# Entry of an expert stage: weights asked for before the search, turns through six banks, upper and lower parts in halves

## The chip, the cores and the metric

One core of a Trainium2 chip. The metric is the device time of one execution in microseconds. TensorE is called PE in the profile, VectorE DVE, ScalarE ACT, GpSimd POOL, and SyncE SP.

## What is computed

One step of a backbone with one layer: 128 context tokens and 2,048 latent tokens of width 1,024. The layer ends in an expert stage in which each of 16 experts chooses its tokens:

```python
cap = CAPACITY_FACTOR * L // N_EXPERTS
affinity = jax.nn.softmax(jnp.einsum('bld,de->ble', h, w_router).astype(jnp.float32), axis=-1)
gate, idx = lax.top_k(jnp.swapaxes(affinity, 1, 2), cap)
xe = jax.vmap(lambda hb, ib: hb[ib])(h, idx)
hid = jax.nn.silu(jnp.einsum('becd,edf->becf', xe, w_gate)) * jnp.einsum('becd,edf->becf', xe, w_up)
ye = jnp.einsum('becf,efd->becd', hid, w_down) * gate[..., None].astype(h.dtype)
return jax.vmap(lambda ib, yb: jnp.zeros((L, D), yb.dtype).at[ib.reshape(-1)].add(yb.reshape(-1, D)))(idx, ye)
```

Here `h` is the token's row after its norm, scaled and shifted. Every expert takes 256 latent tokens and 16 context tokens. All of it is float32.

## The kernel before

The program is a row of stages, each a block with one instruction stream for each engine, and all engines meet at its end. Three matter here. The stage `mixer` stores the normed rows (`normed`) and the rows before the experts (`x2`) to HBM. The stage `selection` finds, by a search of digits on VectorE with small sums on TensorE, which tokens each expert takes, and writes each token's place in `g.pos`. The stage `experts` does the rest; it runs over the 16 experts, the first and the last two written out and the others in a loop.

**An expert in the steady state.** A float32 product is made of three: the weights are split into an upper part `whi` and a lower part `wlo`, the rows into `xhi` and `xlo`, and TensorE adds `whi*xhi`, `whi*xlo` and `wlo*xhi`. The weights of an expert come in 12 chunks of 1 MB (4 of the gate matrix and 4 of the up matrix in turn, then 4 of the down matrix). SyncE's queue loads a chunk into one of three buffers `raw`; it is asked for when `wlo` of the chunk three before it is written. ScalarE copies `raw` to `whi`, VectorE writes `wlo` as `raw` less `whi`; both are rings of four. A product (`product`, 24 matmuls) works off 128 columns of a chunk. For each of 8 tiles `ft` of the hidden width there is a gate product and an up product, then come 8 down products.

**The rows.** For expert `e` VectorE marks in `one_hot(e)`, with 16 compares, which token stands at which place; TensorE adds that up in `compact(e)` (32 small matmuls); VectorE reads the sums in `indices(e)` and writes the row numbers `idx` and the gates. GpSimd's `gather(e)` is two indirect transfers of 512 KB each from `normed` into `xg`; from expert 1 on it also waits until the turns of the expert before are done with `xg`. In `rows_in(e, kk)` TensorE turns (transposes) 128 columns `kk` of the 256 rows, two transposes into a bank of PSUM, and ScalarE (even `kk`) or VectorE (odd `kk`) copies the bank scaled and shifted to `xf`. `rows_high` on ScalarE then copies `xf` to `xhi` in one instruction of 2,048 elements, and `rows_low` on VectorE writes `xlo` in one. In the steady state `rows_in(e + 1, ft)` stands behind the two products of tile `ft` of expert `e`, so TensorE's first turn of expert 1 stands behind its first two products.

**The context rows.** The rows of all 16 experts (256 in all) are gathered at once into `yo`, turned in `context_in` and kept in `kept_c`; each expert copies its 16 from there behind its 256 latent rows.

**The entry.** Ahead of the first product of expert 0 all this happens in the open. TensorE's order: `compact(0)`, `compact_context`, `compact(1)`, then the turns of expert 0 through the two banks `ps_x` (each pair waits until the copy of two pairs before is done) and those of the context rows through the four banks `ps_r`. VectorE's order: `one_hot(0)`, the context's marks, `indices(0)`, `indices_context`, `one_hot(1)`, `split(0, 0)` (the lower part of chunk 0), `indices(1)`, copies, `split(0, 1)`, `rows_low(0)`, `split(0, 2)`. ScalarE's: the upper parts of chunks 0 and 1, copies, `rows_high(0)`, the upper part of chunk 2. SyncE asks for chunks 0 to 2 as the stage begins. The first product waits for `xlo_done`.

The functions as they stand, with their line numbers:

## Time and profile before

| | |
|---|---|
| median of 3 runs | 2353.88 us (2350.2 to 2355.96) |
| profiled execution | 2351.41 us, its span 2349.5 us |
| granted clock of TensorE, mean | 0.958 |
| busy: TensorE, VectorE, ScalarE, GpSimd | 93%, 57%, 43%, 8% |
| DMA | 398.66 MB, mean 170 GB/s |
| `experts` begins | 1048.9 us |
| first product of expert 0 | 1074.96 us |

The trace has one execution. Its times count from the start of the span. A row of the timeline has start and length, engine, line, the tile written and those read, and in brackets how long the engine stood idle before it and what ended that. "SPq" and "POOL DMA_INDIRECT" are issues of transfers, not the transfers. PEclk is the granted clock of TensorE as a share of 2.4 GHz.

### The profile page before, as it was taken

What the parts mean: (1) busy time and instruction counts of PE and PEld (TensorE: products, weight loads), DVE (VectorE), ACT (ScalarE), POOL (GpSimd) and SP (SyncE); (2) the same over time, 40 slices, a digit from 0 to 9 for tenths busy, and PEclk for the clock granted to TensorE, in tenths of its full rate; (3) what the DMA queues carried; (4) which work ended last, traced back from release to release, by engine and by line L of the source; (5) the groups of instructions that cost most, each with busy time, mean ns of one, the idle gap of its engine ahead of it and who ended that gap; (6) DMA issues with size and microseconds to landing.
All of it is one profiled execution on the core that took longest, in us unless ns stands there. A gap on an engine that the chain in (4) does not pass through costs nothing.

```text
span 2349.5 us, 39243 instructions
## 1 busy us (share of the span) xinstructions
PE 2174.3 (93%) x15527; PEld 2010.7 (86%) x15527; DVE 1349.8 (57%) x2079; ACT 999.8 (43%) x1725; POOL 196.0 (8%) x276
## 2 busy tenths in 40 slices
PE   4899999996699999828999999999999999999995
PEld 2878888885588888628999999999999999999995
DVE  2656543407577777475565556555655656565564
ACT  3642221224355555214444444434444444344653
POOL 0000000000011111010000000000000000000112
PEclk8999999998799999858999999999999999999998
DMA  8533343137343444115665666565656665666794
GB/s 288 177 125 133 131 146 125 56 119 239 109 131 129 137 148 148 63 44 189 189 207 166 201 194 202 171 190 187 208 175 188 192 210 167 190 192 201 249 311 158
DMA packets 320348, 398.66 MB, mean 170 GB/s; under 512 B 11631, under 2 KB 273279, under 8 KB 318207
## 3 DMA queue, kind: packets, MB, share of 16 engines
q1 hardware_dynamic: 288990, 287.21, 38.0%
q0 software_dynamic: 24912, 97.53, 13.5%
q10 hardware_dynamic: 6352, 12.65, 1.5%
q8 instruction: 62, 1.02, 0.2%
q14 instruction: 32, 0.25, 0.0%
HBM read 320.22 MB, written 77.14 MB: 169 GB/s over the span
## 4 chain that ended last, share of the span: by engine, by line
PE 48%; DMA 3%; DVE 1%; ACT 1%; issue 1%; POOL 1%; ACTq 0%; DVEq 0%; POOLq 0%
PE experts_ps_r L2380 45%; PE experts_ps_x L2360 1%; PE experts_ps_o L2370 1%; DMA out_y_sample<-experts_xg 1%; DMA out_y_sample<-experts_xf 1%; DMA out_y_sample<-experts_onehot 1%; PE experts_ps_i L2298 0%; ACT experts_whi L2456 0%; DMA x<-experts_yo,experts_idx 0%; ACT experts_junk L2489 0%; DVE experts_wlo L2603 0%; DMA experts_xg<-x,experts_idx 0%; DMA experts_xg<-normed,experts_idx 0%; POOL experts_raw L2264 0%; DVE experts_onehot L2614 0%
## 5 line engine op out<-in xcount | busy, mean ns | idle before, releaser
L2603 DVE TENSOR_TENSOR experts_wlo<-experts_raw,experts_whi 128x2048 fp32r<-128x2048 f32 x192 | 439.9, 2291 | 393.6 <-ACT experts_whi L2456 393.6
L2380 PE MATMUL experts_ps_r<-experts_xhi,experts_whi 128*128 128x272 f32 x2048 | 603.4, 295 | 7.9 <-DVE experts_xlo L2654 5.5
L2380 PE MATMUL experts_ps_r<-experts_xhi,experts_wlo 128*128 128x272 f32 x2048 | 594.1, 290 | 0.0
L2380 PE MATMUL experts_ps_r<-experts_xlo,experts_whi 128*128 128x272 f32 x2048 | 590.8, 288 | 0.0
L2380 PEld LDWEIGHTS experts_ps_r<-experts_xhi,experts_whi 128*128 128x128 f32 x2048 | 387.0, 189 | 8.6 <-DVE experts_xlo L2654 5.7
L2380 PEld LDWEIGHTS experts_ps_r<-experts_xlo,experts_whi 128*128 128x128 f32 x2048 | 387.7, 189 | 0.0
L2380 PEld LDWEIGHTS experts_ps_r<-experts_xhi,experts_wlo 128*128 128x128 f32 x2048 | 386.6, 189 | 0.0
L2456 ACT ACTIVATE experts_whi<-experts_raw 128x2048 fp32r<-128x2048 f32 x192 | 366.1, 1907 | 13.9 <-DMA experts_raw<-in_w_gate 13.1
L2380 PE MATMUL experts_ps_r<-experts_hhi,experts_whi 128*128 128x272 f32 x1024 | 301.3, 294 | 2.0 <-DVE experts_hlo L2767 1.9
L2380 PE MATMUL experts_ps_r<-experts_hhi,experts_wlo 128*128 128x272 f32 x1024 | 296.2, 289 | 0.0
L2380 PE MATMUL experts_ps_r<-experts_hlo,experts_whi 128*128 128x272 f32 x1024 | 294.7, 288 | 0.0
L521 PE MATMUL front_ps<-front_hhi,front_whi 128*128 128x384 f32 (+1 forms) x640 | 236.2, 369 | 0.0
L521 PE MATMUL front_ps<-front_hlo,front_whi 128*128 128x384 f32 (+1 forms) x640 | 230.7, 360 | 0.0
L521 PE MATMUL front_ps<-front_hhi,front_wlo 128*128 128x384 f32 (+1 forms) x640 | 230.6, 360 | 0.0
L2546 ACT ACTIVATE experts_hhi<-experts_hid 128x272 fp32r<-128x272 f32 x128 | 55.2, 431 | 353.8 <-DVE experts_hid L2764 353.8
L2380 PEld LDWEIGHTS experts_ps_r<-experts_hhi,experts_whi 128*128 128x128 f32 x1024 | 192.6, 188 | 5.8 <-DVE experts_hlo L2767 5.6
L2380 PEld LDWEIGHTS experts_ps_r<-experts_hlo,experts_whi 128*128 128x128 f32 x1024 | 193.1, 189 | 0.2 <-issue 0.2
L2380 PEld LDWEIGHTS experts_ps_r<-experts_hhi,experts_wlo 128*128 128x128 f32 x1024 | 192.6, 188 | 0.0
L659 ACT ACTIVATE front_u<-front_ps 128x128 f32<-128x128 f32 (+2 forms) x90 | 40.2, 469 | 247.6 <-PE front_ps L521 227.1
L521 PEld LDWEIGHTS front_ps<-front_hhi,front_whi 128*128 128x128 f32 x640 | 120.8, 189 | 25.4 <-ACT front_u L659 12.6
L521 PEld LDWEIGHTS front_ps<-front_hlo,front_whi 128*128 128x128 f32 x640 | 120.9, 189 | 11.9 <-issue 1.0
L521 PEld LDWEIGHTS front_ps<-front_hhi,front_wlo 128*128 128x128 f32 x640 | 120.7, 189 | 11.8
(474 smaller groups left out, 3169.4 us busy)
## 6 DMA issues: line engine op xcount, KB each, us to landing
experts_raw<-in_w_gate SPq DMA_DIRECT2D x64, 1024.0 KB, 5.0
experts_raw<-in_w_up SPq DMA_DIRECT2D x64, 1024.0 KB, 5.0
experts_raw<-in_w_down SPq DMA_DIRECT2D x64, 1024.0 KB, 5.1
shared_whalf<-in_w_ada SPq DMA_DIRECT2D x16, 1024.0 KB, 5.1
ssd_mz<-mixed SPq DMA_DIRECT2D x17, 768.0 KB, 7.7
mixed<-front_acc POOLq DMA_DIRECT2D x9, 1024.0 KB, 4.2
resid<-early_xin POOLq DMA_DIRECT2D x17, 512.0 KB, 3.2
ssd_xs<-resid SPq DMA_DIRECT2D x17, 512.0 KB, 4.0
```

Source lines behind the costliest of these rows:

```text
L521: mm = pe.matmul(ps[:, out, 0:n], wt[buf][:, kk, :], h[:, kk, t0:t0 + n], start=(kk == 0 and q == 0), stop=(kk == KD - 1 and q == 2))
L659: ins = act.activation(dst_u[:, uo:uo + pn], ps[:, bank_of(s), po:po + pn], func)
L2360: ins = pe.transpose(ps_x[:, kk % 2, P * a:P * a + P], xg[:, a, P * kk:P * kk + P], g.ident[:, :])
L2370: ins = pe.transpose(ps_o[:, P * q:P * q + P], yt[:, 4 * half + q, P * a:P * a + P], g.ident[:, :])
L2380: mm = pe.matmul(dst, w[:, c % RING, kk, cols], r[:, kk, :], start=(kk == 0 and q == 0), stop=(kk == KD - 1 and q == 2))
L2456: act.activation(whi[:, c % RING, :, :], raw[:, c % RAW, :, :], ACT.Copy).then_inc(whi_done, 1)
L2546: act.activation(hhi[:, ft, :], hid[:, ft % 2, :], ACT.Copy).then_inc(hhi_done, 1)
L2603: dve.tensor_tensor(wlo[:, c % RING, :, :], raw[:, c % RAW, :, :], whi[:, c % RING, :, :].bitcast(F32), ALU.subtract).then_inc(wlo_done, 1)
```

## The change

Three things at the entry of `experts`, and one in `indices`.

1. The buffers `raw` and their semaphores are made ahead of `selection`, and SyncE asks for the chunks 0 to 2 in `selection`, as soon as the last rows of `mixer` are stored. `experts` starts with chunk 3.
2. The turns of expert 0 and of the context rows go through one rotation of six banks (`start_bank`: the two of `ps_x`, then the four of `ps_r`), all 8 pairs of expert 0 first, then the 8 of the context; a pair waits for the copy of six pairs before (`bank_free`).
3. The upper and the lower part of expert 0's rows are made in two halves of 1,024 elements (`start_high`, `start_low`), the first between the copies; the context's piece comes by itself (`context_high`, `context_low`). `indices(1)` and `split(0, 1)` stand behind that on VectorE.
4. `indices` writes `idx` ahead of the gates' sums, for every expert.

```diff
         @block.sync
         def _(sp):
+            for sem, value in g.rows_stored:
+                sp.wait_ge(sem, value)
+            for c in range(RAW):
+                w = io[("w_gate", "w_up")[c % 2]][0].rearrange("e (k p) f -> e p k f", p=P)
+                sp.dma_start(g.raw[:, c, :, :], w[0, :, :, CH * (c // 2):CH * (c // 2) + CH]).then_inc(g.w_loaded[c], 16)
...
+        def start_bank(turn):
+            b = turn % 6
+            return ps_x[:, b, :] if b < 2 else ps_r[:, b - 2, :]
...
+            def bank_free(turn):
+                old = turn - 6
+                if 0 <= old < KD:
+                    pe.wait_ge((xf_act, xf_dve)[old % 2], old // 2 + 1)
+                elif old == KD:
+                    pe.wait_ge(ctx_scaled, 1)
+                elif old == KD + 1:
+                    pe.wait_ge(ctx_chain, C_SCALED + 1)
+
+            def start_rows(kk):
+                if kk == 0:
+                    pe.wait_ge(gathered, 32)
+                bank_free(kk)
+                for a in range(2):
+                    ins = pe.transpose(start_bank(kk)[:, P * a:P * a + P], xg[:, a, P * kk:P * kk + P], g.ident[:, :])
+                ins.then_inc(xin_done, 1)
...
             compact(0)
             compact_context()
             compact(1)
-            for kk in range(0, KD + 4, 2):
-                for b in range(2):
-                    if kk < KD:
-                        rows_in(0, kk + b)
-                for b in range(2):
-                    if kk >= 4:
-                        context_in(kk - 4 + b)
+            for kk in range(KD):
+                start_rows(kk)
+            for kk in range(KD):
+                start_context(kk)
             loops(body, pe)
...
+            def start_high(half):
+                act.wait_ge(xf_act, 2 * half + 2)
+                act.wait_ge(xf_dve, 2 * half + 2)
+                kk = slice(4 * half, 4 * half + 4)
+                act.activation(xhi[:, kk, 0:CAP_L], xf[:, kk, :], ACT.Copy).then_inc(xhi_done, 1)
...
             split(0, 0, True)
             split(0, 1, True)
-            for kk in range(0, KD + 4, 2):
-                if kk < KD:
-                    rows_in(0, kk)
-                if kk >= 4:
-                    context_in(kk - 4)
-            rows_high(0)
+            for half in range(2):
+                for kk in (0, 2):
+                    rows_in(0, 4 * half + kk)
+                start_high(half)
+            for kk in range(0, KD, 2):
+                context_in(kk)
+            context_high(0)
             split(0, 2, True)
...
                 idxs.link(dve.tensor_copy(got[:, :, 0:NV], ps_i[:, :, 0:NV]))
+                dve.scalar_tensor_tensor(idx[0][:, :], got[:, :, 0], float(P), got[:, :, 1], ALU.mult, ALU.add
+                                         ).then_inc(idx_done, 1)
                 idxs.link(dve.tensor_tensor(gate[0][:, :], got[:, :, 3], got[:, :, 4], ALU.add))
                 dve.tensor_tensor(gate[0][:, :], gate[0][:, :], got[:, :, 2], ALU.add)
-                dve.scalar_tensor_tensor(idx[0][:, :], got[:, :, 0], float(P), got[:, :, 1], ALU.mult, ALU.add
-                                         ).then_inc(idx_done, 1)
...
+            def start_low(half):
+                dve.wait_ge(xhi_done, half + 1)
+                kk = slice(4 * half, 4 * half + 4)
+                dve.tensor_tensor(xlo[:, kk, 0:CAP_L], xf[:, kk, :], xhi[:, kk, 0:CAP_L].bitcast(F32), ALU.subtract)
...
             one_hot(1)
             split(0, 0)
+            rows_in(0, 1)
+            rows_in(0, 3)
+            rows_in(0, 5)
+            start_low(0)
+            rows_in(0, 7)
+            context_in(1)
+            start_low(1)
+            for kk in (3, 5, 7):
+                context_in(kk)
+            dve.wait_ge(xhi_done, START)
+            context_low(0)
+            split(0, 1)
             indices(1)
-            for kk in range(1, KD + 4, 2):
-                if kk < KD:
-                    rows_in(0, kk)
-                if kk >= 4:
-                    context_in(kk - 4)
-            split(0, 1)
-            rows_low(0)
             split(0, 2)
             loops(body, dve)
```

What this makes of TensorE's order, from the sums of `compact(0)` (`ps_i`) to the first matmul of the first product. Before:

```order
L2298 MATMUL experts_ps_i<-experts_val_e,experts_onehot 128x5 x32
L2306 MATMUL experts_ps_o<-kept_vals,experts_onehot_c 128x80 x2
L2298 MATMUL experts_ps_i<-experts_val_e,experts_onehot 128x5 x32
L2360 MATMUL experts_ps_x<-kept_ident,experts_xg 128x128 x12
L2318 MATMUL experts_ps_r<-kept_ident,experts_yo 128x128 x4
L2360 MATMUL experts_ps_x<-kept_ident,experts_xg 128x128 x4
L2318 MATMUL experts_ps_r<-kept_ident,experts_yo 128x128 x12
L2380 MATMUL experts_ps_r<-experts_xhi,experts_whi 128x272
```

And now:

```order
L2311 MATMUL experts_ps_i<-experts_val_e,experts_onehot 128x5 x32
L2319 MATMUL experts_ps_o<-kept_vals,experts_onehot_c 128x80 x2
L2311 MATMUL experts_ps_i<-experts_val_e,experts_onehot 128x5 x32
L2337 MATMUL experts_ps_x<-kept_ident,experts_xg 128x128 x4
L2337 MATMUL experts_ps_r<-kept_ident,experts_xg 128x128 x8
L2337 MATMUL experts_ps_x<-kept_ident,experts_xg 128x128 x4
L2345 MATMUL experts_ps_r<-kept_ident,experts_yo 128x128 x8
L2345 MATMUL experts_ps_x<-kept_ident,experts_yo 128x128 x4
L2345 MATMUL experts_ps_r<-kept_ident,experts_yo 128x128 x4
L2406 MATMUL experts_ps_r<-experts_xhi,experts_whi 128x272
```

The turns of the context rows (`yo`) no longer stand between those of expert 0 (`xg`), and both are spread over `ps_x` and `ps_r`.

ScalarE, from the upper parts of chunks 0 and 1 (`whi`) to that of chunk 2. Before:

```order
L2456 ACTIVATE experts_whi<-experts_raw 128x2048 x2
L2460 ACTIVATE experts_xf<-experts_ps_x,kept_mod,kept_scale_m 128x256 x3
L2465 ACTIVATE experts_kept_c<-experts_ps_r,kept_mod,kept_scale_m 128x256
L2460 ACTIVATE experts_xf<-experts_ps_x,kept_mod,kept_scale_m 128x256
L2465 ACTIVATE experts_kept_c<-experts_ps_r,kept_mod,kept_scale_m 128x256 x3
L2532 ACTIVATE experts_xhi<-experts_xf 128x8x256
L2533 ACTIVATE experts_xhi<-experts_kept_c 128x8x16
L2456 ACTIVATE experts_whi<-experts_raw 128x2048
```

And now:

```order
L2479 ACTIVATE experts_whi<-kept_raw 128x2048 x2
L2484 ACTIVATE experts_xf<-experts_ps_x,kept_mod,kept_scale_m 128x256
L2484 ACTIVATE experts_xf<-experts_ps_r,kept_mod,kept_scale_m 128x256
L2560 ACTIVATE experts_xhi<-experts_xf 128x4x256
L2484 ACTIVATE experts_xf<-experts_ps_r,kept_mod,kept_scale_m 128x256
L2484 ACTIVATE experts_xf<-experts_ps_x,kept_mod,kept_scale_m 128x256
L2560 ACTIVATE experts_xhi<-experts_xf 128x4x256
L2489 ACTIVATE experts_kept_c<-experts_ps_r,kept_mod,kept_scale_m 128x256 x2
L2489 ACTIVATE experts_kept_c<-experts_ps_x,kept_mod,kept_scale_m 128x256
L2489 ACTIVATE experts_kept_c<-experts_ps_r,kept_mod,kept_scale_m 128x256
L2566 ACTIVATE experts_xhi<-experts_kept_c 128x8x16
L2479 ACTIVATE experts_whi<-kept_raw 128x2048
```

One upper part of the rows (`xhi` from `xf`) of 8x256 has become two of 4x256, one of them ahead of half of the copies; the context's piece (8x16) is last as before.

VectorE, from the last instruction of `indices(1)` before (the row numbers `idx`) to the lower parts of chunks 2 and 3. Before:

```order
L2628 SCALAR_TENSOR_TENSOR experts_idx<-experts_got 128x2
L2648 TENSOR_SCALAR experts_xf<-experts_ps_x,kept_scale_m,kept_mod 128x256 x3
L2697 TENSOR_SCALAR experts_kept_c<-experts_ps_r,kept_scale_m,kept_mod 128x256
L2648 TENSOR_SCALAR experts_xf<-experts_ps_x,kept_scale_m,kept_mod 128x256
L2697 TENSOR_SCALAR experts_kept_c<-experts_ps_r,kept_scale_m,kept_mod 128x256 x3
L2603 TENSOR_TENSOR experts_wlo<-experts_raw,experts_whi 128x2048
L2653 TENSOR_TENSOR experts_xlo<-experts_xf,experts_xhi 128x8x256
L2654 TENSOR_TENSOR experts_xlo<-experts_kept_c,experts_xhi 128x8x16
L2603 TENSOR_TENSOR experts_wlo<-experts_raw,experts_whi 128x2048 x2
```

And now, from the second half of `xlo` on:

```order
L2694 TENSOR_TENSOR experts_xlo<-experts_xf,experts_xhi 128x4x256
L2740 TENSOR_SCALAR experts_kept_c<-experts_ps_r,kept_scale_m,kept_mod 128x256
L2740 TENSOR_SCALAR experts_kept_c<-experts_ps_x,kept_scale_m,kept_mod 128x256
L2740 TENSOR_SCALAR experts_kept_c<-experts_ps_r,kept_scale_m,kept_mod 128x256
L2697 TENSOR_TENSOR experts_xlo<-experts_kept_c,experts_xhi 128x8x16
L2637 TENSOR_TENSOR experts_wlo<-kept_raw,experts_whi 128x2048
L2668 COPY experts_idx<-experts_idx 128x2
L2669 COPY experts_gate<-experts_gate 128x2
L2659 COPY experts_got<-experts_ps_i 128x2x5
L2660 SCALAR_TENSOR_TENSOR experts_idx<-experts_got 128x2
L2662 TENSOR_TENSOR experts_gate<-experts_got 128x2
L2663 TENSOR_TENSOR experts_gate<-experts_gate,experts_got 128x2
L2637 TENSOR_TENSOR experts_wlo<-kept_raw,experts_whi 128x2048 x2
```

The lower part of chunk 1 (`wlo`) stood ahead of `xlo` and now stands behind it; the six instructions of `indices(1)` (two copies of `idx` and `gate`, `got`, `idx`, two sums) stood ahead of all copies and now stand behind that `wlo`. GpSimd's gather for expert 1 waits for the `idx` among them.

## Rows read from the trace of the kernel before

**Rows 1.** The page, part 1: engine, busy us, share of the span, instructions.

```profile
PE 2174.3 (93%) x15527; PEld 2010.7 (86%) x15527; DVE 1349.8 (57%) x2079; ACT 999.8 (43%) x1725; POOL 196.0 (8%) x276
```

**Rows 2.** TensorE's waits, 1082 to 2290 us: total us, times, longest us.

```profile
PE experts_ps_r L2380 <- DVE experts_wlo L2603: 2.5, 2, 2.2
PE experts_ps_r L2380 <- DVE experts_hlo L2767: 1.7, 1, 1.7
```

**Rows 3.** The timeline, 1054 to 1063 us: start, us, engine, line, instruction.

```profile
1054.10 1.91 ACT L2456 ACTIVATE experts_whi<-experts_raw 128x2048 fp32r<-128x2048 f32 x1 [13.11 <-DMA experts_raw<-in_w_gate]
...
1054.13 0.15 DVE L2628 SCALAR_TENSOR_TENSOR experts_idx<-experts_got 128x2 uint32<-128x2 f32 x1
...
1055.15 1.04 POOL L2196 DMA_INDIRECT experts_xg<-normed,experts_idx  x1 [50.16 <-DVE experts_idx L2628]
...
1056.77 1.91 ACT L2456 ACTIVATE experts_whi<-experts_raw 128x2048 fp32r<-128x2048 f32 x1 [0.76 <-DMA experts_raw<-in_w_up]
...
1056.89 3.30 DVE L2614 TENSOR_SCALAR experts_onehot<-kept_slots,experts_pos_e 128x256 bf16<-128x256 bf16 x16
...
1060.03 2.29 DVE L2603 TENSOR_TENSOR experts_wlo<-experts_raw,experts_whi 128x2048 fp32r<-128x2048 f32 x1
...
1060.25 1.01 PE L2298 MATMUL experts_ps_i<-experts_val_e,experts_onehot 128*128 128x5 bf16 x32 [6.30 <-DVE experts_onehot L2614]
...
1062.04 0.71 PEld L2360 LDWEIGHTS experts_ps_x<-kept_ident,experts_xg 128*128 128x128 f32 x4 [0.87 <-DMA experts_xg<-normed,experts_idx]
...
1062.77 0.56 ACT L2460 ACTIVATE experts_xf<-experts_ps_x,kept_mod,kept_scale_m 128x256 f32<-128x256 f32 x1 [4.08 <-PE experts_ps_x L2360]
```

**Rows 4.** The timeline, 1068 to 1075 us, up to the first product.

```profile
1068.31 0.95 POOL L2196 DMA_INDIRECT experts_xg<-normed,experts_idx  x1 [8.16 <-PE experts_ps_x L2360]
...
1068.44 1.70 DVE L2697 TENSOR_SCALAR experts_kept_c<-experts_ps_r,kept_scale_m,kept_mod 128x256 f32<-128x256 f32 x3 [0.24 <-PE experts_ps_r L2318]
...
1070.27 1.91 ACT L2532 ACTIVATE experts_xhi<-experts_xf 128x2048 fp32r<-128x2048 f32 x1 [0.55 <-DVE experts_kept_c L2697]
...
1072.41 2.29 DVE L2653 TENSOR_TENSOR experts_xlo<-experts_xf,experts_xhi 128x2048 fp32r<-128x2048 f32 x1
...
1072.50 0.37 SPq L2177 DMA_DIRECT2D experts_raw<-in_w_gate  x1
...
1074.62 0.28 DVE L2654 TENSOR_TENSOR experts_xlo<-experts_kept_c,experts_xhi 128x128 fp32r<-128x128 f32 x1
...
1074.96 0.59 PE L2380 MATMUL experts_ps_r<-experts_xhi,experts_whi 128*128 128x272 f32 x1 [5.47 <-DVE experts_xlo L2654]
```

**Rows 5.** DMA queues, 1056.8:1058.4, 1058.6:1061.6, 1069.8:1074.2: packets, MB, share of 16 engines.

```profile
q1 hardware_dynamic: 603, 0.62, 108.4%
...
q0 software_dynamic: 326, 1.21, 98.3%
...
q0 software_dynamic: 286, 1.05, 75.3%
```

**Rows 6.** Windows: stretch, busy us of each engine, PEclk, DMA share, GB/s.

```profile
990.00:1000.00 10.00, 10.00 (x48) 10.00 (x48) 3.11 (x9) 0.43 (x1) 2.52 (x9) 0.50 0.00 1
```

**Rows 7.** The timeline, first turns of expert 1, and expert 2's index and gather.

```profile
1082.72 0.38 PE L2360 MATMUL experts_ps_x<-kept_ident,experts_xg 128*128 128x128 f32 x2
...
1088.99 0.38 PE L2360 MATMUL experts_ps_x<-kept_ident,experts_xg 128*128 128x128 f32 x2
...
1149.08 0.15 DVE L2628 SCALAR_TENSOR_TENSOR experts_idx<-experts_got 128x2 uint32<-128x2 f32 x1
...
1149.51 0.95 POOL L2196 DMA_INDIRECT experts_xg<-normed,experts_idx  x1 [79.00 <-DVE experts_idx L2628]
```

**Rows 8.** Windows, 1070 to 1080 us, for the granted clock (PEclk).

```profile
1070.00:1072.00 2.00, 0.00 (x0) 0.00 (x0) 1.97 (x2) 1.73 (x1) 0.51 (x1) 0.94 0.88 254
1072.00:1074.00 2.00, 0.00 (x0) 0.00 (x0) 2.00 (x2) 2.00 (x3) 0.00 (x0) 0.50 0.88 275
...
1078.00:1080.00 2.00, 2.00 (x16) 2.00 (x15) 0.00 (x0) 0.11 (x1) 0.00 (x0) 0.85 0.92 290
```

More of the change, by code:

```diff
@@ L2159, in experts @@
         C_GATED = 4
+        START = 3
         C_SAVED, C_SSQ = 17, 25
@@ L2172, in body @@
                 for c in range(NCH):
+                    if first and c < RAW:
+                        continue
                     w, col = (wd, c - 8) if c >= 8 else ((wg, wu)[c % 2], c // 2)
-                    if not (first and c < RAW):
-                        hold(sp, settled, (wlo_done, e * NCH + (c - RAW + 1)))
+                    hold(sp, settled, (wlo_done, e * NCH + (c - RAW + 1)))
                     src = w[bass.ds(e, 1), :, :, CH * col:CH * col + CH].rearrange("o p k f -> (o p) k f")
@@ L2308, in compact_context, with start_context @@
                 mm.then_inc(ctx_turned, 1)
-            def context_in(kk):
+            def bank_free(turn):
[13 more added lines that the diff above has]
+                ins.then_inc(xin_done, 1)
+            def start_context(kk):
                 if kk == 0:
                     pe.wait_ge(ctx_moved, 32)
-                if kk >= 4 and kk % 2 == 0:
-                    pe.wait_ge(ctx_scaled, kk // 2 - 1)
-                elif kk >= 4:
-                    pe.wait_ge(ctx_chain, C_SCALED + kk // 2 - 1)
+                bank_free(KD + kk)
                 for h in range(2):
-                    ins = pe.transpose(ps_r[:, kk % 4, P * h:P * h + P], yo[:, h, P * kk:P * kk + P], g.ident[:, :])
+                    ins = pe.transpose(start_bank(KD + kk)[:, P * h:P * h + P], yo[:, h, P * kk:P * kk + P], g.ident[:, :])
                 ins.then_inc(ctx_turned, 1)
@@ L2356, in rows_in @@
                     pe.wait_ge(gathered, e * 32 + 32)
-                if not (first_tiles(e, 1) and kk < 2):
-                    pe.wait_ge((xf_act, xf_dve)[kk % 2], e * 4 + kk // 2)
+                pe.wait_ge((xf_act, xf_dve)[kk % 2], e * 4 + kk // 2)
                 for a in range(2):
@@ L2459, in rows_in @@
                 act.wait_ge(xin_done, e * 8 + (kk + 1))
-                act.activation(xf[:, kk, :], ps_x[:, 0, 0:CAP_L], ACT.Identity,
+                src = start_bank(kk) if first_tiles(e, 1) else ps_x[:, 0, :]
+                act.activation(xf[:, kk, :], src[:, 0:CAP_L], ACT.Identity,
                                scale=g.scale_m[:, kk, 1:2], bias=g.mod[:, SH_M + kk, 1:2]).then_inc(xf_act, 1)
@@ L2528, in rows_high, with context_high @@
                 act.wait_ge(xf_dve, e * 4 + 4)
+                act.activation(xhi[:, :, 0:CAP_L], xf[:, :, :], ACT.Copy)
+                context_high(e)
+            def start_high(half):
[3 more added lines that the diff above has]
+                act.activation(xhi[:, kk, 0:CAP_L], xf[:, kk, :], ACT.Copy).then_inc(xhi_done, 1)
+            def context_high(e):
                 if first_tiles(e, 1):
@@ L2647, in rows_in, with context_low @@
                 dve.wait_ge(xin_done, e * 8 + (kk + 1))
-                dve.tensor_scalar(xf[:, kk, :], ps_x[:, 1, 0:CAP_L], g.scale_m[:, kk, 1:2],
+                src = start_bank(kk) if first_tiles(e, 1) else ps_x[:, 1, :]
+                dve.tensor_scalar(xf[:, kk, :], src[:, 0:CAP_L], g.scale_m[:, kk, 1:2],
                                   g.mod[:, SH_M + kk, 1:2], ALU.mult, ALU.add).then_inc(xf_dve, 1)
             def rows_low(e):
-                dve.wait_ge(xhi_done, e + 1)
+                dve.wait_ge(xhi_done, e + START)
                 dve.tensor_tensor(xlo[:, :, 0:CAP_L], xf[:, :, :], xhi[:, :, 0:CAP_L].bitcast(F32), ALU.subtract)
+                context_low(e)
+            def start_low(half):
+                dve.wait_ge(xhi_done, half + 1)
+                kk = slice(4 * half, 4 * half + 4)
+                dve.tensor_tensor(xlo[:, kk, 0:CAP_L], xf[:, kk, :], xhi[:, kk, 0:CAP_L].bitcast(F32), ALU.subtract)
+            def context_low(e):
                 dve.tensor_tensor(xlo[:, :, CAP_L:ROWS], kept_c[:, :, bass.ds(e, 1), :].rearrange("p k o c -> p k (o c)"),
@@ L2696, in context_in @@
                 dve.wait_ge(ctx_turned, C_IN + kk + 1)
-                step(dve.tensor_scalar(kept_c[:, kk, :, :].rearrange("p e c -> p (e c)"), ps_r[:, kk % 4, 0:NE * CAP_C],
+                step(dve.tensor_scalar(kept_c[:, kk, :, :].rearrange("p e c -> p (e c)"), start_bank(KD + kk)[:, 0:NE * CAP_C],
                                        g.scale_m[:, kk, 0:1], g.mod[:, SH_M + kk, 0:1], ALU.mult, ALU.add),
@@ L2863, in build @@
         g.gm_rows = k.sb("gm_rows", [P, 2, D])
+        g.raw, g.w_loaded = k.sb("raw", [P, RAW, KD, CH]), k.sems("w_loaded", RAW)
         g.slots = k.sb("slots", [P, CAP_L], BF16)
```

8 lines of the change are left out of this document (4 added, 4 removed).

## The prediction

> **What bounds the kernel now.** I read the page first: TensorE works for 93% of the span [rows 1]. Then the waits of TensorE from 1082 us to 2290 us, the loop over the experts: two releasers, 4.2 us in all [rows 2]. So from the first products on TensorE is the bound, everything behind it follows at its pace, and what the change does to the time is by how much earlier TensorE runs once its stream is steady, that is behind the first rows of expert 1. The entry has one long wait: the first product stands still for 5.47 us until `xlo` is written and starts at 1074.96 [rows 4].
>
> Third view, the timeline of the entry. Its chain of last waits is: VectorE's 16 compares of `one_hot(1)` from 1056.89 to 1060.19; `compact(1)` on TensorE, 1060.25 to 1061.26; a gap of 0.78 us, which the landing of expert 0's gathered rows ends, and turns from 1062.04 [rows 3]; copies out of the turned rows, the last three of them context copies of VectorE, 1068.44 to 1070.14; the whole upper part on ScalarE, 1.91 us from 1070.27; the whole lower part on VectorE, 2.29 us from 1072.41, then its context piece at 1074.62; the product [rows 4]. From the first turn to the first product it is 12.9 us.
>
> **The weights, fetched early.** Three transfers of 1 MB leave the entry. ScalarE's 13.11 us and 0.76 us of waiting for them go [rows 3], but are worth nothing by themselves: ScalarE is through both upper parts at 1058.68 and has its first rows at 1062.77 [rows 3]. What they did cost is the queue: from 1056.8 to 1058.4 the 16 DMA engines move only weights, and the gathers (software queue) move from 1058.6 on, though the first was issued at 1055.15 [rows 3, 5]. The undisturbed gather of expert 1 is issued at 1068.31 and its megabyte is moved from 1069.8 to 1074.2, all but a few packets: 1.5 us to the first byte, 5.9 us from the first issue to the end [rows 4, 5]. So gather 0 now ends near 1055.15 − 0.28 (the index is written before the gate sums, two links earlier) + 5.9 = 1060.8, before `compact(1)` ends at 1061.26. The turns start there, 0.78 us earlier. At their new place, before the search, the transfers meet DMA engines that are idle from 990 to 1000, and VectorE works 3.11 of those 10 us [rows 6]; there I cost them at 0, and at 3.1 us if VectorE took twice as long beside them, which no row suggests.
>
> **The turns and the halves.** Transposes issue every 0.18 us (four in 0.71 us) [rows 3], a pair in 0.36. With six banks none of the first six pairs waits. Copies cost 0.56 us on ScalarE and 1.70 / 3 = 0.57 on VectorE [rows 3, 4]; a half of the upper part is taken as 1.91 / 2 = 0.96 or a little more, a half of the lower as 1.15 [rows 4]. First rows reach ScalarE 0.73 us after the first transpose [rows 3], so:
> - ScalarE: copy 0 at 1062.0, copy 2 at 1062.7; VectorE: `wlo` 0 until 1062.3 (now with no `indices(1)` behind it), copy 1 at 1062.4, copy 3 at 1063.1.
> - Upper half 0 from 1063.7 to 1064.7; ScalarE copies 4 and 6 until 1065.8. VectorE: copy 5 until 1064.4, lower half 0 from 1064.8 to 1065.9, copy 7 until 1066.5, context copy 1 until 1067.0.
> - Upper half 1 from 1066.5 to 1067.5, lower half 1 from 1067.55 to 1068.7, then context copies 3, 5, 7 on VectorE until 1070.4. ScalarE's context copies 0, 2, 4, 6 end at 1069.8 and lie beside them; turns 14 and 15 wait for context copy 0, done at 1068.1, and are not last.
> - Context piece of the upper part 0.3 us, of the lower one from 1070.8; the product follows 0.34 us after that start, as now (1074.62 to 1074.96) [rows 4]: **1071.15**.
>
> That is 3.8 us earlier: 0.8 from the turns' start, 3.0 from halves that lie beside the turns. The first product needs `wlo` 0 alone; the second needs `wlo` 1, now split behind `xlo`, 1071.0 to 1073.3, long before the first product (over 4 us at the low clock) ends. Chunk 4 of the weights is then asked for at 1073.3 in place of 1072.50 [rows 4]; its first product is the ninth, four pairs of 6.3 us [rows 7] behind the first.
>
> **What is late next.** `indices(1)` moved behind `split(0, 1)`. Before, gather 1 waited 8.16 us for the turns and was issued at 1068.31 [rows 4]. Now its index waits for VectorE: 1073.3 plus two small copies, `got` and the index, 0.15 to 0.2 us each, so the index starts at 1073.7; in the loop the gather follows 0.43 us behind (1149.08 to 1149.51) [rows 7]: **issued at 1074.15, 5.8 us later than before**. TensorE's third step, the first turn of expert 1, waits for it. In the trace of before that turn stands at 1082.72, 7.76 us behind the first product [rows 4, 7]; now TensorE is there at 1078.9. The gather alone would land at 1074.15 + 5.9 = 1080.05. But chunk 4, issued 0.85 us ahead of it, needs 2.7 us of all engines (0.62 MB in 1.6 us) [rows 5]; if the software queue stands back for it as it did at 1056.8, the first rows move from about 1077.3 and then 1 MB takes some 3.3 us (the four gathers moved 1.21 MB in 3.0) [rows 5]: 1080.6. I take 1080.6, since that queueing is what the trace shows. TensorE then waits 1.7 us.
>
> So the sum is not 3.8 us. Whatever the entry gives, TensorE goes on at the landing: 1082.72 − 1080.6 = 2.1 us. Bounds: 1080.05 gives 2.7 us; if chunk 5, asked for at 1076.4, shares the engines too, all three megabytes end near 1074.5 + 3 × 2.7 = 1082.6 and nothing is left of the gain.
>
> The Trainium skill says (DMA: Bandwidth & Descriptors, SWDGE vs HWDGE vs iDMA) that each DMA engine goes round-robin between its software and hardware queues. By that, gather 1 would share with chunk 4 and land about 1080.1, a gain of 2.6 us, or near 1082.6 if chunk 5 shares with it. The trace speaks against it at one place: no software packet in the 1.6 us of [rows 5].
>
> **The clock.** In the windows the granted clock is 0.94 from 1070 to 1072, 0.50 (1.2 GHz) from 1072 to 1074, and 0.85 from 1078 to 1080, back at 2.4 GHz some 3.5 us into the products [rows 8], and TensorE stood idle from the last turn, near 1069.5, to 1074.96. The low clock costs: first pair of products 7.76 us, the second with its turn 6.27 (1082.72 to 1088.99) [rows 4, 7], so 1.5 us and the turn, some 1.7. The new idle time before the products is about 2.7 us instead of 5.5. Were the clock still high there, TensorE would only reach the gather earlier and wait longer: worth nothing. What counts is whether it falls in the wait for gather 1: then up to 1.7 us are lost behind it. The Trainium skill warns of such waits in a stream of products (TensorE: Matmul & The Clock Gate, HAM oscillation). A wait of 1.7 us between 7.8 us of work and more work is short beside the idle time that lowered it here, so I leave it out of the sum.
>
> **Rivals.**
> - *Gather 1 is in time, or nearly* (landing by 1079.2): 3.6 us or so faster, about 2350.2. For it: the DMA engines have little else. Against it: even undisturbed it takes 5.9 us. Chance 0.13.
> - *The gather wait outruns the entry's gain* (the other side): it lands behind 1082.7, because both chunks go ahead of it or POOL starts as late as after the first index (1.02 us behind it, 1054.13 to 1055.15 [rows 3]), and the clock falls in the 3.8 us of waiting. At 1082.8 and with 1.7 us of low clock it is +1.8 us, 2355.7. It decides from a landing of 1082.7, or of 1081.0 with the clock low. Chance 0.17.
> - *The fetch does not do its work*, because `compact(1)` and not the gather starts the turns: it is worth 0.8 us at most in any case; without it the first product is at 1071.9 and the sum is the same, as the landing of gather 1 rules. It can't be told in the time. Chance 0.1, at 2351.8.
> - *Forecast*: 2.1 us faster. Chance 0.5. The rest, 0.1, is for what the moved buffer and the new places of waits do elsewhere.
>
> **How the numbers follow.** The profiled execution took 2351.41 us (span 2349.5 and 1.9 around it); by the sum it would take 2349.3. The median of the three runs is 2353.88, 2.5 us above it, so the forecast is 2353.9 − 2.1 = 2351.8. The three runs lie 5.8 us apart, so a median of three may be off by 2 us by itself. The range goes from 2348 (2350.2 less 2) to 2356 (2355.7). A measurement here tells about 0.3%, 7 us, from no change. The largest gain that any case has is 3.8 + 1.7 = 5.5 us, with the clock high from the first product and no wait; so faster by more than that has 0.04, slower 0.02, no difference 0.94.
>
> **What the new profile would show.** Right: no wait of ScalarE for weights at the entry; turns from 1061.3 on that clock; two half upper parts of about 1 us between the copies; first product 9.9 us behind the first turn; gather 1 issued 3 us behind the first product's start; TensorE idle 1 to 2.5 us at the first turn of expert 1, released by that gather; that turn 9.5 us behind the first product. Wrong: a gather that lands inside the first two products (then the gain is 3.8), a first product later than 1072.5 (then a copy waits on a bank that I took for free), a low clock behind the wait, or a longer search.

## The result, and the profile after

The changed kernel takes 2356.88 us (median of 16 runs), the kernel before, beside it on the same chips, 2351.05 us. The ratio is 1.0022, interval [1.0015, 1.0029]: some 5 us slower, where 2 us faster was forecast. The forecast of 2351.8 us was built on a median of three runs, 2353.88, which lies 2.8 us above that of the sixteen; against the sixteen it would have been 2349.0, and further off. The profiled executions took 2358.11 us (span 2356.3) and 2351.41 us (span 2349.5).

TensorE's waits from 1082 to 2290 us answer to [rows 2]:

```profile
PE experts_ps_x L2386 <- DMA experts_xg<-normed,experts_idx: 5.0, 1, 5.0
PE experts_ps_r L2406 <- DVE experts_wlo L2637: 2.2, 1, 2.2
PE experts_ps_r L2406 <- DVE experts_hlo L2810: 1.7, 1, 1.7
```

The longest of each of the two old waits is unchanged. A third has come: once, 5.0 us, for the gathered rows of expert 1. The timeline from the turns to the second turn of expert 1 answers to [rows 3, 4, 7]:

```profile
1066.52 1.12 PE L2337 MATMUL experts_ps_x<-kept_ident,experts_xg 128*128 128x128 f32 x4 [1.10 <-DMA experts_xg<-normed,experts_idx]
...
1069.17 1.06 ACT L2560 ACTIVATE experts_xhi<-experts_xf 128x1024 fp32r<-128x1024 f32 x1 [0.51 <-DVE experts_xf L2683]
...
1070.26 1.22 DVE L2694 TENSOR_TENSOR experts_xlo<-experts_xf,experts_xhi 128x1024 fp32r<-128x1024 f32 x1 [0.33 <-ACT experts_xhi L2560]
...
1076.89 0.59 PE L2406 MATMUL experts_ps_r<-experts_xhi,experts_whi 128*128 128x272 f32 x1 [2.31 <-DVE experts_xlo L2697]
...
1079.42 0.16 DVE L2660 SCALAR_TENSOR_TENSOR experts_idx<-experts_got 128x2 uint32<-128x2 f32 x1
...
1079.77 2.28 DVE L2637 TENSOR_TENSOR experts_wlo<-kept_raw,experts_whi 128x2048 fp32r<-128x2048 f32 x1
...
1079.85 3.02 POOL L2209 DMA_INDIRECT experts_xg<-normed,experts_idx  x1 [15.54 <-DVE experts_idx L2660]
...
1083.17 0.94 POOL L2209 DMA_INDIRECT experts_xg<-normed,experts_idx  x1 [0.31 <-issue]
...
1089.89 0.69 PE L2386 MATMUL experts_ps_x<-kept_ident,experts_xg 128*128 128x128 f32 x2 [5.04 <-DMA experts_xg<-normed,experts_idx]
...
1098.16 0.38 PE L2386 MATMUL experts_ps_x<-kept_ident,experts_xg 128*128 128x128 f32 x2
```

Times in a trace drift by what lies ahead, so I count from VectorE's first instruction of the stage `experts` (1048.94 us before, 1053.35 after). The start of the turns is then +13.10 before and +13.17 after; the first product +26.02 and +23.54; the first issue of gather 1 +19.37 and +26.50; the first turn of expert 1 +33.78 and +36.54; its second turn +40.05 and +44.81. The next turns come 6.27 us apart in both. So the entry does give 2.48 us at the first product, and TensorE is 4.76 us behind two pairs later.

Two more things are to be seen. The first issue of the gather takes 3.02 us in place of 0.95 [rows 4]: it lies beside `split(0, 2)`, a VectorE instruction of 2.28 us that reads `raw` and `whi`. And SyncE asks for chunk 4 ahead of this issue, and for chunk 5 while it runs:

```profile
1079.06 0.37 SPq L2190 DMA_DIRECT2D kept_raw<-in_w_gate  x1
1082.08 0.37 SPq L2190 DMA_DIRECT2D kept_raw<-in_w_up  x1
```

The DMA queues of 1082:1084, 1084:1086, 1086:1088 and 1088:1090 us (packets, MB, share), as in [rows 5], the first of the four with hardware packets alone:

```profile
q1 hardware_dynamic: 696, 0.70, 104.0%
...
q1 hardware_dynamic: 696, 0.71, 105.4%
q0 software_dynamic: 6, 0.02, 3.3%
...
q0 software_dynamic: 168, 0.63, 79.4%
q1 hardware_dynamic: 178, 0.17, 24.7%
...
q1 hardware_dynamic: 330, 0.34, 51.5%
q0 software_dynamic: 114, 0.39, 48.5%
```

In the four us from 1082 almost nothing but weights moves: 1.4 MB of them, and 6 packets of rows, all six behind 1085.5. The rows then take 4.4 us, until TensorE goes on at 1089.89, and share with what is left of chunk 5 and, asked for at 1086.42, chunk 6. The windows show the granted clock (last but two) in the wait and behind it:

```profile
1084.00:1086.00 2.00, 0.85 (x7) 0.63 (x5) 1.90 (x1) 0.07 (x1) 0.11 (x1) 1.00 1.09 369
1086.00:1088.00 2.00, 0.00 (x0) 0.00 (x0) 1.18 (x3) 0.43 (x1) 0.00 (x0) 0.86 1.04 401
1088.00:1090.00 2.00, 0.11 (x1) 0.11 (x2) 0.00 (x0) 0.00 (x0) 0.00 (x0) 0.50 1.00 363
1090.00:1092.00 2.00, 2.00 (x10) 2.00 (x11) 0.00 (x0) 0.56 (x1) 0.00 (x0) 0.50 0.98 327
1092.00:1094.00 2.00, 2.00 (x10) 2.00 (x10) 0.00 (x0) 0.00 (x0) 0.00 (x0) 0.50 0.09 30
1094.00:1096.00 2.00, 2.00 (x16) 2.00 (x16) 0.00 (x0) 0.40 (x1) 0.00 (x0) 0.93 0.00 0
```

It falls from 2.4 to 1.2 GHz in the wait and stays there for the first 4 us of the next products: from the first turn to the second it takes 8.27 us, where it took 6.27 [rows 7].

### The profile page after: what moved, and what is told of

The parts are those of the page before. It is cut to its first block, busy times and chain, and to the rows that moved or that the text cites. A ratio compares the mean times of both kernels' runs of the same rounds, so it can differ in the third digit from the quotient of the medians.

```text
span 2356.3 us, 39263 instructions
## 1 busy us (share of the span) xinstructions
PE 2175.1 (92%) x15527; PEld 2011.4 (85%) x15527; DVE 1349.5 (57%) x2080; ACT 999.3 (42%) x1726; POOL 198.0 (8%) x276
## 4 chain that ended last, share of the span: by engine, by line
PE 48%; DMA 3%; DVE 1%; ACT 1%; issue 1%; POOL 1%; ACTq 0%; DVEq 0%; POOLq 0%
PE experts_ps_r L2406 45%; PE experts_ps_x L2386 1%; PE experts_ps_o L2396 1%; DMA out_y_sample<-experts_xg 1%; DMA out_y_sample<-experts_onehot 1%; DMA out_y_sample<-experts_xf 1%; DMA experts_xg<-normed,experts_idx 1%; PE experts_ps_i L2311 0%; ACT experts_whi L2479 0%; DMA x<-experts_yo,experts_idx 0%; ACT experts_junk L2513 0%; DVE experts_wlo L2637 0%; DMA experts_xg<-x,experts_idx 0%; POOL kept_raw L2277 0%; POOL experts_xg L2209 0%
## 5 line engine op out<-in xcount | busy, mean ns | idle before, releaser
L2637 DVE TENSOR_TENSOR experts_wlo<-kept_raw,experts_whi 128x2048 fp32r<-128x2048 f32 x192 | 439.9, 2291 | 390.1 <-ACT experts_whi L2479 390.1
L2479 ACT ACTIVATE experts_whi<-kept_raw 128x2048 fp32r<-128x2048 f32 x192 | 366.1, 1907 | 7.9 <-PEq L1780 7.9
```

What stands on the lines that cost most here:

```text
L2479: act.activation(whi[:, c % RING, :, :], raw[:, c % RAW, :, :], ACT.Copy).then_inc(whi_done, 1)
L2637: dve.tensor_tensor(wlo[:, c % RING, :, :], raw[:, c % RAW, :, :], whi[:, c % RING, :, :].bitcast(F32), ALU.subtract).then_inc(wlo_done, 1)
```

## The experiments

**Theory:** the loss is the index of expert 1 behind `split(0, 1)`. Its gather comes out late, is stretched by VectorE, stands behind chunks 4 and 5, and the wait lowers the clock. **Rivals:** the early fetch or the turns cost something by themselves; a part of the theory (issue, chunk, clock) does no harm. All times below are of one profiled execution each, counted from the beginning of `experts`; the ratios are of all timed runs. An interval reaches 2 to 3 us to either side (1.6 for the changed kernel), so the ratios tell e1 and e11 from the changed kernel, but not e5, e6 or e8; what those show is read from their traces.

| kernel | first product | first issue, its length | first turn of expert 1 (wait) | second turn | ratio |
|---|---|---|---|---|---|
| before | 26.02 | 19.37, 0.95 | 33.78 (0) | 40.05 | 1 |
| changed | 23.54 | 26.50, 3.02 | 36.54 (5.04) | 44.81 | 1.0022 |
| e1_index_first | 23.07 | 17.13, 1.35 | 30.85 (0) | 37.12 | 0.9992 |
| e11_index_first_again | 23.31 | 17.10, 1.63 | 30.72 (0) | 36.99 | 0.9985 |
| e3_fetch_only | 26.02 | 19.50, 0.95 | 33.70 (0) | 39.97 | 1.0000 |
| e4_turns_only | 24.86 | 27.83, 3.02 | 37.94 (4.78) | 46.51 | 1.0033 |
| e7_index_first_no_fetch | 24.03 | 18.09, 1.35 | 32.57 (0) | 38.85 | 1.0000 |
| e2_vector_holds | 24.08 | 27.05, 3.02 | 37.17 (4.48) | 46.06 | 1.0029 |
| e5_chunk5_later | 23.03 | 26.00, 3.01 | 34.56 (3.76) | 43.30 | 1.0014 |
| e6_hold_by_memset | 22.93 | 25.89, 0.95 | 33.46 (2.70) | 41.31 | 1.0010 |
| e10_hold_and_later | 23.61 | 26.58, 0.94 | 34.23 (1.82) | 40.56 | 1.0005 |
| e8_index_between | 23.12 | 23.88, 3.01 | 35.03 (4.08) | 44.01 | 1.0025 |
| e9_index_late_alone | 25.92 | 26.95, 2.75 | 36.51 (2.64) | 44.33 | 1.0013 |

How far one execution can be trusted: the changed kernel, e2, e5, e6 and e10 have the same instructions up to the first product, and it stands at 22.93 to 24.08. Differences of 1 us between two rows of the table in that column are no finding by themselves. The waits for expert 1's rows and the pairs behind them differ by more.

**The index back in its place (e1, and e11 the same again).** In VectorE's stream of the changed kernel:

```
             split(0, 0)
+            indices(1)
             rows_in(0, 1)
...
             split(0, 1)
-            indices(1)
             split(0, 2)
```

> The changed kernel with one call moved: indices(1) stands on VectorE right behind split(0, 0), ahead of the copies, as in the kernel before. Late-index theory (the whole loss comes from the row numbers of expert 1 standing behind split(0, 1)): gather 1 is issued as soon as the turns of expert 0 are done, some 17 us behind the stage's begin in place of 26.5, is landed when TensorE comes to its first turn of expert 1, and the wait of 5.04 us there and the low clock behind it (2.0 us) are gone; the second turn of expert 1 stands 38 us behind the stage's begin (44.8 in the changed kernel, 40.05 before), the time is 6 to 7 us under the changed kernel, some 1 to 2 us under the kernel before (2350). Rival, early fetch in the way: the search is 1.2 us longer in the changed kernel, and if that is the fetch it stays, so no gain over the kernel before is left (ratio 1.000). Rival, six banks and halves themselves cost: the time stays above the kernel before by 3 us or more.

> The changed kernel with indices(1) back directly behind split(0, 0), a second time, beside the two others on one chip. Theory (the 2.9 us by which its first steady products are ahead reach the end): 0.9985 to 0.9992. Rival (nothing reaches the end, and the first comparison of 0.9992 was scatter): 0.9998 to 1.0003.

Measured: 0.9992 [0.9983, 1.0001] (2348.76 us), and 0.9985 [0.9975, 0.9995] (2349.01 us). The interval of e1 alone just holds 1, that of e11 does not. In e1 GpSimd issues right behind the turns of expert 0, and TensorE's first turn of expert 1 comes without a wait:

```profile
1066.62 1.35 POOL L2209 DMA_INDIRECT experts_xg<-normed,experts_idx  x1 [6.29 <-PE experts_ps_x L2337]
1068.28 0.94 POOL L2209 DMA_INDIRECT experts_xg<-normed,experts_idx  x1 [0.30 <-issue]
...
1068.87 1.23 DVE L2694 TENSOR_TENSOR experts_xlo<-experts_xf,experts_xhi 128x1024 fp32r<-128x1024 f32 x1 [0.81 <-ACT experts_xhi L2560]
...
1080.34 0.38 PE L2386 MATMUL experts_ps_x<-kept_ident,experts_xg 128*128 128x128 f32 x2
```

With that one move undone the rest of the change is worth 2.9 to 3.1 us at the second turn (37.12 and 36.99 against 40.05). The ratios give 1.9 and 3.5 us (0.1% of the time is 2.4 us), so it reaches the end. This is the fastest version of the study.

**One part alone.** e3 is the kernel before with nothing but the three transfers asked for ahead of the search; e4 is the changed kernel with them asked for at the beginning of `experts` as before; e7 is e1 with them there.

> The kernel before with the early fetch of chunks 0 to 2 alone. My forecast gave it 0.8 us at the start of the turns; the changed kernel's trace shows its turns 13.17 us behind the stage's begin, before 13.10, so I expect nothing from it there now: turns at 12.9 to 13.2 us. If the fetch makes the search longer: 61.4 us from the first instruction of the selection to the experts' begin in place of 60.3, and 1 us slower (ratio 1.0005). If that 1.2 us is the clock's doing: same as before within 0.5 us.

> The changed kernel without its early fetch: chunks 0 to 2 are asked for as the experts begin, as in the kernel before. The fetch alone measured 1.000 of the kernel before, so I expect the loss unchanged: within 1.5 us of the changed kernel (ratio 1.001 to 1.003 to the kernel before), the wait for gather 1 at 4.5 to 5.5 us. Rival (only fetch and turns together lose): the ratio is 0.999 or less.

> The six banks and the halves with indices(1) at its old place, and no early fetch. If the fetch is worth nothing, it does what the same kernel with the fetch did (second turn of expert 1 at 37.1 us behind the stage's begin, ratio 0.999): 37.0 to 37.6. If the early fetch brought part of that, the turns start 0.3 us or more later than 12.70 us behind the begin and the ratio is nearer 1.000.

Measured: 1.0000 [0.9990, 1.0010], 1.0033 [1.0020, 1.0047] and 1.0000 [0.9990, 1.0010]. The fetch costs nothing that can be seen, and with the old order of turns it gives nothing. With the new turns the first product is 1.3 us earlier in the changed kernel than in e4 (23.54 and 24.86) and 1.0 earlier in e1 than in e7: without the fetch TensorE waits 2.46 and 1.62 us for the first gathered rows, with it 1.10 and 0.67. That is no more than kernels with one and the same entry differ by (22.93 to 24.08; e2, with the fetch, is behind e7, without), so a gain near 1 us is likely and not shown. For e7 the second of its two cases came: turns at 13.65, second turn 38.85, where 37.0 to 37.6 stood for a fetch that is worth nothing. The loss is in e4 too, so it is not the fetch's. The fourth part of the change, `idx` ahead of the gates' sums, was not tried alone; the first issue of gather 0 comes at +5.95 in place of +6.21.

**The same fault put into the kernel before (e9).** Only this, in its VectorE stream:

```
             split(0, 0)
-            indices(1)
...
             rows_low(0)
+            indices(1)
             split(0, 2)
```

> The kernel before, with its order of turns and one whole upper and lower part kept and no early fetch; only indices(1) stands between rows_low(0) and split(0, 2) instead of behind split(0, 0). Theory (the late index is the whole loss, and it needs no other part of the change): the first product stays at 26.0 us behind the beginning of experts; the index is written near 26.3, the first issue of gather 1 begins near 26.7 and takes 3.0 us beside split(0, 2); chunk 4 (asked for at 23.6) is through, chunk 5 (asked for near 29) goes ahead; the rows land near 34.5 to 35, TensorE waits 0.8 to 1.5 us for them where it waited none, the second turn of expert 1 is 41 to 43 (before 40.05), ratio 1.0005 to 1.0015. Rival (the index is late only against an early first product): it lands before 33.8, no wait, second turn at 40.0, ratio 1.0000.

Measured: 1.0013 [1.0003, 1.0023]; the wait is 2.64 us, longer than the 0.8 to 1.5 expected, and the second turn 44.33.

```profile
1075.45 2.28 DVE L2603 TENSOR_TENSOR experts_wlo<-experts_raw,experts_whi 128x2048 fp32r<-128x2048 f32 x1
...
1075.80 2.75 POOL L2196 DMA_INDIRECT experts_xg<-normed,experts_idx  x1 [15.75 <-DVE experts_idx L2628]
1078.86 0.94 POOL L2196 DMA_INDIRECT experts_xg<-normed,experts_idx  x1 [0.30 <-issue]
...
1085.36 0.69 PE L2360 MATMUL experts_ps_x<-kept_ident,experts_xg 128*128 128x128 f32 x2 [2.64 <-DMA experts_xg<-normed,experts_idx]
1093.18 0.38 PE L2360 MATMUL experts_ps_x<-kept_ident,experts_xg 128*128 128x128 f32 x2
```

The late index alone makes the kernel before slower, by 3 us. Wait (2.64) and low clock (7.82 us for the pair in place of 6.27) are all but the whole of its 4.3 us at the second turn. The rival falls.

**The stretched issue (e2, e6).** VectorE is to stand still ahead of `split(0, 2)` until GpSimd has issued the gather. In e2 GpSimd signals with an empty instruction, in e6 with a small one that writes:

```
             gather(1)
+            pool.nop().then_inc(settled, 1)                  # e2
+            pool.memset(flag[:, :], 0.0).then_inc(settled, 1)  # e6 in its place
...
             indices(1)
+            dve.wait_ge(settled, 2)
             split(0, 2)
```

> The changed kernel, but VectorE stands still behind indices(1) until GpSimd has issued both halves of gather 1, and only then splits chunk 2; so chunk 5 is also asked for later. Theory of the blocked issue (the first issue of gather 1 took 3.02 us in place of 0.95 because VectorE ran its two-input instruction of 2.28 us beside it): both issues take 0.95 to 1.0, the rows land about 33.5 us behind the stage's begin in place of 36.5, TensorE waits 1.5 to 2.5 us in place of 5.04, and the clock probably stays high; the time is 3 to 5 us under the changed kernel. Rival, queueing alone (the 3.02 us is how the profile shows a full queue of transfers): the first issue stays at 3 us.

> The changed kernel, but behind gather 1 GpSimd writes one small tile, and VectorE waits for that write before it splits chunk 2 (the earlier attempt signalled with an instruction that ran ahead of the issues and held nothing). Theory of the blocked issue: both issues of gather 1 now take 0.95 to 1.0 us instead of 3.02 and 0.94; VectorE's next split starts 28.8 to 29.5 us behind the stage's begin, chunk 5 is asked for near 31, and the rows land behind chunk 4 alone, near 32.5 to 33.5 (36.5 in the changed kernel); TensorE waits 1.5 to 2.5 us. With the clock high behind the wait the time is 5 us under the changed kernel, with the clock low 3. Rival (the length of the issue is the queue's, not VectorE's): it stays at 3 us.

e2 held nothing (1.0029 [1.0018, 1.0040]): the empty instruction's signal came before the issues, `split(0, 2)` began ahead of them, and the first still took 3.02 us. e6 did hold (1.0010 [1.0001, 1.0020]):

```profile
1081.10 0.95 POOL L2210 DMA_INDIRECT experts_xg<-normed,experts_idx  x1 [15.03 <-DVE experts_idx L2662]
1082.36 0.95 POOL L2210 DMA_INDIRECT experts_xg<-normed,experts_idx  x1 [0.30 <-issue]
1083.30 0.11 POOL L2249 MEMSET experts_flag<- 128x1 f32 x1
...
1083.45 4.49 DVE L2639 TENSOR_TENSOR experts_wlo<-kept_raw,experts_whi 128x2048 fp32r<-128x2048 f32 x2 [2.35 <-POOL experts_flag L2249]
```

Both issues take 0.95 us, and the wait for the rows falls from 5.04 to 2.70 us. Chunk 4 was under way in both kernels, so the long issue was VectorE's doing and not the queue's. The clock fell behind this wait too, so of the two times forecast the 3 us under the changed kernel came (2.8 by the ratios). The hold also puts chunk 5 behind the gather, since it is asked for when `split(0, 2)` is done.

**Chunk 5 behind the gather (e5), and both together (e10).**

```
                     hold(sp, settled, (wlo_done, e * NCH + (c - RAW + 1)))
+                    if first and c == 5:
+                        sp.wait_ge(gathered, 64)
```

> The changed kernel, but SyncE asks for chunk 5 only when gather 1 has landed. Queue theory (gather 1's packets stood behind chunks 4 and 5 on the DMA engines): the first issue is still 3 us long, but packets of the gather move from 1.5 us behind it, 33 us from the stage's begin, and land near 34 to 34.5; TensorE waits 2.5 to 3 us in place of 5.04 and the time is 2 to 4 us under the changed kernel. If the blocked issue alone makes it late, nothing changes (within 1 us).

> The changed kernel with both cures: VectorE holds split(0, 2) until GpSimd has issued gather 1 (issues of 0.95 and 0.95 us), and chunk 5 is asked for only when the rows of expert 1 have landed. Held alone, the landing was 33.5 us behind the beginning of experts and the wait 2.70 us; chunk 5 later alone, 34.6 and 3.76. Theory (issue and chunk each hold the rows up by themselves): first product at 22.9, landing at 31.3 to 32.3, wait 0.6 to 1.6 us. Rival (with the issue early, chunk 5 came behind the gather anyhow): landing at 33.4 as with the hold alone, wait 2.6. On the clock: if the fall behind the wait comes with a wait of any length here, the second pair of products takes 7.8 us again and the second turn is near 39.7; if a wait of about 1 us is too short, the pair takes 6.3 and the turn is near 38.2, 1.8 us ahead of before (40.05). Ratio 0.9990 to 1.0000.

e5: 1.0014 [1.0005, 1.0023]. From the first product to the first turn it takes 11.53 us, 13.00 in the changed kernel: chunk 5 (and chunk 6, for which SyncE asks behind it) held the rows up by 1.5 us, behind an issue still of 3.01. The wait of 3.76 us is longer than the 2.5 to 3 expected. e10: 1.0005 [0.9995, 1.0015]. There it takes 10.62 us, in e6 10.53: with a short issue chunk 5 comes last anyhow, and waiting longer with it gives nothing. The theory that the two add up falls, its rival holds. The first pair took 8.80 us in e10 (low clock for longer) and 7.83 in e6, so TensorE waited 1.82 us only, and behind that the clock did not fall:

```profile
1079.00:1081.00 2.00, 0.42 (x4) 0.20 (x2) 2.00 (x2) 0.00 (x0) 0.00 (x0) 1.00 0.49 199
1081.00:1083.00 2.00, 1.76 (x14) 1.76 (x15) 0.76 (x2) 0.93 (x2) 0.00 (x0) 1.00 0.28 53
1083.00:1085.00 2.00, 2.00 (x18) 2.00 (x17) 0.00 (x0) 0.26 (x1) 0.00 (x0) 1.00 1.02 349
```

The pair behind it takes 6.33 us. Behind the 2.70 us of e6 it takes 7.85, behind 2.64 in e9 7.82, behind 3.76 in e5 8.74, behind 4.08 in e8 8.98, behind 4.48 in e2 8.89, behind 4.78 in e4 8.57, behind 5.04 in the changed kernel 8.27. e10 differs from these by more than its wait, since its first pair ran longer at the low clock.

**The index one place earlier (e8)**, between `context_low(0)` and `split(0, 1)`.

> The changed kernel with indices(1) between context_low(0) and split(0, 1), so 2.3 us earlier than in it and 10 us later than in the kernel before. Theory: the first issue of gather 1 is stretched to 3 us again, now by split(0, 1), but is over near 27.3 us behind the begin, ahead of chunk 4's transfer; the rows land near 31.5 to 32.5, just at TensorE's turn (31.3 behind the begin), which waits 0 to 1.5 us. The time is 4 to 6 us under the changed kernel, within 1.5 us of the one with the index first. Rival (lateness costs in proportion): the wait falls by 2.3 us alone, to 2.7.

Measured: 1.0025 [1.0015, 1.0036], no better than the changed kernel; the expectation was wrong. The index comes 2.6 us earlier, but now two lower parts follow it back to back, and both issues lie beside them. The rows come 1.5 us earlier (+35.03), and of that the pair behind the wait takes half back (8.98 us, 8.27 in the changed kernel):

```profile
1072.44 4.49 DVE L2637 TENSOR_TENSOR experts_wlo<-kept_raw,experts_whi 128x2048 fp32r<-128x2048 f32 x2
...
1072.53 3.01 POOL L2209 DMA_INDIRECT experts_xg<-normed,experts_idx  x1 [13.03 <-DVE experts_idx L2660]
1075.85 1.90 POOL L2209 DMA_INDIRECT experts_xg<-normed,experts_idx  x1 [0.30 <-issue]
```

The Trainium skill (SBUF — State Buffer, Who interferes with whom) says that a VectorE instruction with two inputs in SBUF contends with a GpSimd instruction that reads SBUF. The traces agree where VectorE came first: the issue takes 3.01 or 3.02 us when a 2.28 us instruction began 0.08 or 0.09 us ahead of it, 0.95 us with VectorE standing still (e6). The same section tells of a probe in which `tensor_tensor`, this very kind of instruction, did not hold up a transfer issued by GpSimd; here it did, by 2.07 us. Where the issue came first neither was held up: in e1 the second one began at 1068.28 and took 0.94 us, and the lower part that began inside it at 1068.87 took its usual 1.23.

## Why the prediction was wrong

- **"Landing near 1080.6, TensorE waits 1.7 us": this step failed.** By my count that is 9.5 us behind the first product. It was 13.0, and the wait 5.04. Chunk 4 ahead of the rows was right. Three terms were wrong. The length of the issue had no term: it stood in the sum as in rows where it began with no two-input instruction of VectorE under way, 0.95 us [rows 4, 7]; beside `split(0, 2)` it took 2.07 more. Chunk 5, asked for meanwhile, went ahead of the rows, which the prediction had set aside as a bound. With both gone the way is 10.5 us (e6), with the long issue alone 11.5 (e5), with both 13.0: 1.0 and 1.5 us. That the long issue is what let chunk 5 pass is likely from the times (1082.08, ahead of the issue's end at 1082.87), but e6 holds back issue and chunk together, so it is not shown. The last 1.1 us, from 9.5 to 10.5, is a wrong sum: I took 3.3 us to move the rows from 1.21 MB in 3.0 us [rows 5], which gives 2.5 for 1 MB, while the undisturbed gather took 4.4 (1069.8 to 1074.2, in the prediction itself). In e6 the rows move from some 3.3 us behind the issue, near the 3.15 forecast, and take 4.3; in the changed kernel they take 4.4. Sharing by turns between the two queues, the other way of reckoning that stood in the prediction, did not show from 1082 to 1086.
- **The clock behind the wait** was left out of the sum as too short a wait. For a wait of 1.7 us the one near it bears that out (1.82 us in e10: 6.33 us). At 5.04 us it cost 2.0 us. The rival on the other side (chance 0.17) had both chunks ahead of the rows and the clock low behind 3.8 us of waiting, +1.8 in all; the mechanism is that rival's, but for the long issue, and it measured +4.8.
- **The turns' start, 0.78 us earlier:** it was 0.07 later. I priced gather 0 by gather 1's 5.9 us; it took 7.22 (1059.30 to 1066.52). It doesn't move alone: from 1060 to 1066.5 the software queue moved 1.50 MB, and gather 0 is 1.05 of them; the rest is the context's. And in the kernel before it took 6.89 (1055.15 to 1062.04), with the weights still in the queue, so there was little to gain. e3 shows no gain from the fetch; what e4 and e7 show is 1.0 and 1.3 us, within the scatter.
- **From the first turn to the product, 9.9 us:** 10.37, in place of 12.92 [rows 3, 4]. The halves took 1.06 and 1.22 us, for 0.96 and 1.15. So the first product was 2.5 us earlier, not 3.8; e1 has 2.9.
- **Right:** no wait of ScalarE for weights at the entry, halves beside the turns, the landing of gather 1 as what rules the sum, gather 1 issued 3.0 us behind the product's start, the queue that serves weights first. "The gather is the bound" was right, and its price decided the sign.

The sum over what was measured: at the second turn, the gain of 2.5 at the first product, less 5.04 of wait, less 2.0 of clock, less 0.2 of the first pair, is −4.8; the ratio gives −5.2. Through the table the ratio rises with the second turn, but for e8 and e9, whose intervals hold what their turns would give (4.0 and 4.3 us, 1.0017 and 1.0018). The profiles' own times can't be compared directly, for two reasons. Ahead of `experts` the search took 59.6, 60.3 or 61.3 to 61.5 us (59.6, 60.3 and 61.3 in e2, e5 and e6, which share all of its code). The three longest (changed, e6, e8) all have the early fetch, but six others with it are at 59.6 or 60.3; whether it has a part stays open. And from the second turn to the end of the span it takes 1254.7 us in e9 and 1264.2 in e4; 6.4 of these 9.5 us are one wait of TensorE near the end of the last expert, for the rows `yt` of ScalarE:

```profile
PE experts_ps_x L2351 <- ACT experts_yt L2562: 1.3, 1, 1.3
...
PE experts_ps_x L2369 <- ACT experts_yt L2586: 7.7, 1, 7.7
```

The first line is e9's, the second e4's. The wait is 4.9 us before, 4.0 in the changed kernel, 3.4 in e1 and 7.7 in e11, which is e1's code again: what sets it stays open.

## What to carry to other kernels

Before an instruction is moved in order to be out of the way, look at what it feeds on another engine's queue, and at what runs beside that issue in its new place. An indirect transfer behind a two-input VectorE instruction is both late and slow to issue; put the index ahead of it (here 2.9 us gained in place of 4.8 lost). Price the wait of a product stream with the clock behind it: here 1.8 us cost 1.8 (e10), 2.6 us cost 4.2 (e9). Take the time that a transfer's bytes need from a row of the same kind of transfer, undisturbed (here 4.4 us, in place of 3.3).
